# Two transformer blocks on one core: the opening with the first three input-projection units abreast, and another order of its first fetches

## What is computed

```python
# first block
cs = jax.nn.silu(c)
mod = cs @ w_ada[l] + b_ada[l]
shift1, scale1, gate1, shift2, scale2, gate2 = [m[:, None, :] for m in jnp.split(mod, 6, axis=-1)]
h = _rmsnorm(x, norm1_g[l]) * (1.0 + scale1) + shift1
proj = h @ w_in[l]
...
# second block: keys and values of its memory, which depend on nothing in the first block
mem_n = rmsnorm(mem, g_mem)
k_m, v_m = jnp.split(mem_n @ w_mem_kv, 2, axis=-1)
k = rmsnorm(k_m.reshape(bsz, m, MEM_HEADS, MEM_HEAD_DIM), memk_gain)
```

## Time and profile before

| | |
|---|---|
| median of three runs | 814.39 us (814.33 to 815.30) |
| the profiled execution's own time | 814.49 us |
| its span, first to last instruction | 812.7 us |
| TensorE busy | 800.6 us, 99% |
| VectorE busy | 625.6 us, 77% |
| ScalarE busy | 439.7 us, 54% |
| mean granted TensorE clock | 0.998 |

### The profile page before, as it was taken

One profiled execution on the slowest core, in us unless ns is written; L12 is line 12 of the kernel. 1 busy time (PEld: TensorE's weight loads), 2 busy tenths in 40 slices (PEclk: granted clock), 3 DMA queues, 4 the chain that ended last, 5 costly groups with the idle time before them and its releaser, 6 DMA issues.

```text
span 812.7 us, 14321 instructions
## 1 busy us (share of the span) xinstructions
PE 800.6 (99%) x5970; PEld 759.5 (93%) x5970; DVE 625.6 (77%) x913; ACT 439.7 (54%) x603; POOL 33.2 (4%) x32
## 2 busy tenths in 40 slices
PE   7899999999999999999999999999999999999998
PEld 7899789999999999999878999999999999999998
DVE  5998999888888887676977686644787876777765
ACT  7838667637555344444857546654436544545351
POOL 1000000000000000000000000000000121111210
PEclk9999999999999999999999999999999999999999
DMA  9996848964536865555454543444444655455501
GB/s 357 423 417 221 356 161 308 360 260 156 211 140 241 310 251 201 202 187 177 156 192 137 190 163 149 156 152 160 156 155 163 237 203 177 162 206 202 177 31 52
DMA packets 25487, 168.99 MB, mean 208 GB/s; under 512 B 2896, under 2 KB 3408, under 8 KB 5840
## 3 DMA queue, kind: packets, MB, share of 16 engines
q1 hardware_dynamic: 25280, 168.08, 56.1%
q10 hardware_dynamic: 144, 0.01, 0.0%
HBM read 167.03 MB, written 1.05 MB: 207 GB/s over the span
## 4 chain that ended last, share of the span: by engine, by line
PE 84%; DVE 9%; DMA 3%; ACT 2%; issue 1%; SPq 0%; DVEq 0%; ACTq 0%
PE ps L1648 57%; PE ps L1679 13%; PE ps L1682 7%; DVE wlo L1001 3%; PE ps L1712 3%; DMA raw<-in_w_in 2%; ACT whi L473 2%; PE ps L1890 1%; PE ps L1861 1%; PE ps L1862 1%; DMA raw<-in_first_unit 1%; PE ps L1923 1%; DVE raw L976 0%; DVE tmp L1570 0%; DVE x L1506 0%
## 5 line engine op out<-in xcount | busy, mean ns | idle before, releaser
L1001 DVE TENSOR_TENSOR wlo<-raw,whi 128x2048 fp32r<-128x2048 f32 (+1 forms) x130 | 290.4, 2239 | 85.8 <-ACT whi L473 82.4
L473 ACT ACTIVATE whi<-raw 128x2048 fp32r<-128x2048 f32 (+2 forms) x140 | 250.7, 1799 | 100.9 <-PE ps L1682 67.0
L1648 PE MATMUL ps<-h_two,whi 128*128 128x256 f32 x1344 | 247.2, 286 | 2.5 <-DVE wlo L1001 2.1
L1648 PEld LDWEIGHTS ps<-h_two,whi 128*128 128x128 f32 x1344 | 210.7, 193 | 4.9 <-DVE wlo L1001 2.3
L1648 PE MATMUL ps<-h_two,wlo 128*128 128x256 f32 x672 | 190.7, 284 | 0.0
L1648 PEld LDWEIGHTS ps<-h_two,wlo 128*128 128x128 f32 x672 | 129.5, 193 | 0.0
L1648 PE MATMUL ps<-fhi,whi 128*128 128x256 f32 x352 | 99.6, 283 | 0.0
L1648 PE MATMUL ps<-flo,whi 128*128 128x256 f32 x352 | 99.6, 283 | 0.0
L1648 PE MATMUL ps<-fhi,wlo 128*128 128x256 f32 x352 | 99.6, 283 | 0.0
L1648 PEld LDWEIGHTS ps<-fhi,wlo 128*128 128x128 f32 x352 | 67.6, 192 | 0.0
L1648 PEld LDWEIGHTS ps<-fhi,whi 128*128 128x128 f32 x352 | 67.6, 192 | 0.0
(11 more groups left out here) (260 smaller groups left out, 1328.2 us busy)
## 6 DMA issues: line engine op xcount, KB each, us to landing
raw<-in_w_up SPq DMA_DIRECT2D x44, 1024.0 KB, 4.8
raw<-in_w_in SPq DMA_DIRECT2D x43, 1024.0 KB, 4.8
raw<-in_w_down SPq DMA_DIRECT2D x22, 1024.0 KB, 4.8
raw<-in_w_ada SPq DMA_DIRECT2D x14, 1024.0 KB, 5.4
raw<-in_branches SPq DMA_DIRECT2D x10, 1024.0 KB, 5.4
raw<-in_w_out SPq DMA_DIRECT2D x4, 1024.0 KB, 7.3
raw<-in_w_o SPq DMA_DIRECT2D x4, 1024.0 KB, 4.8
raw<-in_w_mem_kv SPq DMA_DIRECT2D x3, 1024.0 KB, 9.0
```

The lines of the kernel that those rows point to most:

```text
L473: return nc.scalar.activation(dst, src, func, **kw)
L1001: V.tensor_tensor(wlo[:, w % SPLIT, c:UNIT], raw[:, slot, c:UNIT], f32(whi[:, w % SPLIT, c:UNIT]), ALU.subtract).then_inc(raw_done, 1)
L1648: ins = mm(out_, l, r, start=start and i == 0, stop=stop and i == 2, **kw)
```

## The change

Four things are edited, all in the opening; the same computation is done, by the same instructions but for one unit's split.

- `START_PLAN`: unit 3 is fetched ahead of piece 1, and unit 5 ahead of piece 3.
- `HALVED` takes in unit 6 (`WIN1 + 2`), so that ScalarE rounds it in two instructions and VectorE subtracts in two.
- `START_STEPS`: units 4, 5 and 6 do their tiles 0 to 2 one unit after the other, then all three do tile 3, then unit 7 does its tiles 0 to 3. Before, only units 4 and 5 did so, and unit 6 did its four tiles after them.
- ScalarE's and VectorE's lists follow suit: unit 3 is rounded ahead of `memory_keys`, unit 5 is subtracted ahead of piece 3, and ScalarE's `first_tile(4)` stands ahead of the rounding of unit 7 and no longer behind it.

```diff
@@ -76,9 +76,9 @@
 
 FIRST = 4
 MEMKV, WIN1, BR1, WO1, FFN1 = 0, 4, 21, 25, 29
-START_PLAN = [("w", 0), ("w", 1), ("w", 2), ("ada", 0), ("ada", 1), ("w", 3), ("ada", 2), ("w", 4), ("ada", 3), ("w", 5),
+START_PLAN = [("w", 0), ("w", 1), ("w", 2), ("ada", 0), ("w", 3), ("ada", 1), ("ada", 2), ("w", 4), ("w", 5), ("ada", 3),
               ("w", 6), ("ada", 4), ("w", 7), ("ada", 5), ("ada", 6), ("ada", 7), ("ada", 8)]
-HALVED = (MEMKV + 1, MEMKV + 2, MEMKV + 3, WIN1 + 3, WIN1 + FIRST, WIN1 + FIRST + 1)
+HALVED = (MEMKV + 1, MEMKV + 2, MEMKV + 3, WIN1 + 2, WIN1 + 3, WIN1 + FIRST, WIN1 + FIRST + 1)
 WIN2, BR2, WO2, FFN2 = 62, 88, 94, 98
 NW = 131
 PLAN, RAW_OF = build_plan()
@@ -118,8 +118,7 @@
 SCORE_BANK, PT_BANKS, PV_BANK = 4, (3, 6), 7
 TURN_BANK = 4
 ROWS_BANK = 4
-START_STEPS = ([(0, kt) for kt in range(3)] + [(1, kt) for kt in range(3)] + [(0, 3), (1, 3)]
-               + [(2, kt) for kt in range(4)] + [(3, kt) for kt in range(4)]
+START_STEPS = ([(w, kt) for w in range(3) for kt in range(3)] + [(w, 3) for w in range(3)] + [(3, kt) for kt in range(4)]
                + [(w, kt) for kt in (4, 5, 6, 7) for w in range(FIRST)])
 
 NORMS = {"mem": (KT, 0, 3, 3), "one": (KT, 0, 6, 6), "two": (KT, 0, 4, 4), "final": (KT, 0, 3, 6), "mix": (KT, 0, 3, 3),
@@ -606,25 +605,25 @@
             act.wait_ge(sem("one_rstd"), 1)
             for tt in range(NT):
                 copy(xn[:, tt, :], xt[:, tt, :], scale=rstd[:, c_one + tt:c_one + tt + 1]).then_inc(sem("xn_ready"), 1)
+            round_unit(MEMKV + 3)
             memory_keys(0)
             memory_keys(1)
-            round_unit(MEMKV + 3)
             act.wait_ge(sem("vec_landed"), 16)
             first_tile(0)
-            first_tile(1)
             act.wait_ge(emptied["act"], EVACUATED[MEMKV + 1][1])
             copy(memk_sq[:, :, :], kmem[:, :, :], ACT.Square).then_inc(sem("memk_sq"), 2)
+            first_tile(1)
+            memory_values(0)
             round_unit(WIN1)
             first_tile(2)
-            memory_values(0)
             round_unit(WIN1 + 1)
             memory_values(1)
-            first_tile(3)
-            round_unit(WIN1 + 2)
             act.wait_ge(sem("memk_mean"), 1)
             copy(memk_saved, ps[:, NORMS["memk"][2], 0:8]).then_inc(sem("memk_saved"), 1)
+            round_unit(WIN1 + 2)
+            first_tile(3)
+            first_tile(4)
             round_unit(WIN1 + 3)
-            first_tile(4)
             act.wait_ge(sem("lam_dots"), 2)
             copy(lam_e, lam_d, ACT.Exp).then_inc(sem("lam_exp"), 1)
             first_tile(5)
@@ -1136,17 +1135,20 @@
             invert("one")
             dve.wait_ge(sem("cs_ready"), 1)
             first_gain(0)
+            split_low(MEMKV + 3, fold=False)
             first_gain(1)
-            split_low(MEMKV + 3, fold=False)
             first_low(0)
+            first_gain(2, 0)
             first_low(1)
-            first_gain(2)
+            first_gain(2, 1)
             split_low(WIN1, fold=False)
             first_low(2)
-            first_gain(3)
             split_low(WIN1 + 1, fold=False)
+            first_gain(3, 0)
+            split_low(WIN1 + 2, fold=False, half=0)
+            first_gain(3, 1)
+            split_low(WIN1 + 2, fold=False, half=1)
             first_low(3)
-            split_low(WIN1 + 2, fold=False)
             first_gain(4)
             split_low(WIN1 + 3, fold=False, half=0)
             first_low(4)
```

## The result

The changed kernel takes 817.85 us (median of five runs, 817.66 to 818.34) against 814.39, a ratio of 1.0047 with a 95% interval of 1.0036 to 1.0057. The profiled execution took 818.34 us, 3.85 more than the one of before (814.49).

The account below looks back on a forecast made before the run. TensorE, busy 99%, bounds the kernel; unit 8's start is the measure. Unit 7 at 49.3, 17 steps to 61.5, slow stretch to 63.3, plus 2.46 gives 65.8, +2.6: 817.0 us, range 814.2 to 818.9.

Parts of the forecast that it names:

- The walk to unit 7: TensorE's opening: waits of 0.7, 0.4 and 0.7 us, then a 3.7 us pause until unit 7 at 49.3.
- low 7: VectorE's low part of tile 7, in its tail: expected at 60.4, which is 57.99 + 2.4.
- the price of the one slow stretch seen before: TensorE behind the pause before unit 7: the clock falls once more, costing 1.76 us as before.
- the stated bounds of 0 and 3.5: Limits on the slow stretch's cost: 0 if the clock stays up, 3.5 us if low twice as long.
- the 65.8 of the sum: Start of unit 8 on TensorE: 63.3 for unit 4's end plus 2.46, against 63.19 before, so +2.6.
- The clock stayed up: Rival, TensorE behind unit 7's pause: no slow stretch, VectorE's 64.4 sets unit 8, +1.2, 815.6 us; chance 0.15.
- The transfers landed in their new order: Rival, opening fetches: transfers don't land in issue order, unit 5 lands at 35.7, +4.4, 818.8 us; chance 0.07.
- The gain case: Rival, opening: unit 7's half ready before about 48.2, pause only 1.3 us, 813.3 us or less; chance 0.11.
- the 62.1: Start of unit 8 in the rival where the opening gains: 57.99 + 2.8 + 1.2, or -1.1.
- taken up later: Rival, chain after 63.19: spare time there absorbs a late unit 8, 814.4 us; chance 0.07.

Follow-up runs that it names:

- the first two experiments: Changed kernel with ScalarE rounding unit 7 ahead of tile 4: 813.89 us, 0.9999 of before; kernel before with tile 4 ahead of that rounding: 817.20 us, 1.0034.
- the first experiment: Changed kernel with one line moved back, so ScalarE rounds unit 7 ahead of tile 4: 813.89 us, 0.9999 of before.

## Why the prediction was right, and where it was off

**The walk to unit 7 held.** The wait before unit 3 went. The next waits came out at 0.35, 0.80 and 0.51 us for 0.7, 0.4 and 0.7, the pause before unit 7 at 3.44 for 3.7, its end at 49.65 for 49.3, VectorE's idle time at 2.03 for 2.2, low 7 at 60.64 for 60.4. That ScalarE's order makes this pause was shown from both sides, by the first two experiments.

**The clock was mis-sized.** I took the price of the one slow stretch seen before, 1.76 us; it cost 14.91 - 12.24 = 2.67 this time, inside the stated bounds of 0 and 3.5. The stretch was 6.8 us long and not 3.4; about 1.3 of it lay in the pause and cost nothing. With 0.35 for the start of unit 7 and 0.91 for the clock, the 65.8 of the sum becomes 67.06; measured 67.03. Where the clock fell is told by a finer stretch:

```profile
48.00:50.00 2.00, 0.35 (x1) 0.35 (x2) 1.63 (x3) 1.98 (x3) 0.00 (x0) 0.58 1.03 430
```

It was at 1.2 GHz for 2 x 0.42 x 2 = 1.7 of these 2 us, so from 48.3, and unit 7 began at 49.65. In time: 817.85 against 817.0, the range (814.2 to 818.9) and the sign held. The median is nearer to the forecast than unit 8 is, because the profiled execution was the slowest of the five, 0.49 above it.

**The base was not one number.** The profiled execution of before belongs to the group with the slow stretch (median 814.70), and I took it for all. So the forecast rested the fall of the clock on one execution in which it fell, where, by their mean clocks, it stayed up in 38 of 72; that it fell in all five of the changed kernel is more than the rows of before could tell. Against the other group (813.48) the changed kernel is 4.4 us slower.

**The rivals.** The clock stayed up in none of the changed kernel's five runs (mean clock 0.998 in two, at 817.66 and 817.85, and 0.996 in three, at 817.81 to 818.34); forced up, it gives 815.91, where this rival stood at 815.6. The transfers landed in their new order: ScalarE rounded unit 3 at 23.10, and its only wait for DMA between units 4 and 7 was the one for unit 6. The gain case needed unit 7's half by 48.2; moved there (TensorE began unit 7 at 47.54 in the first experiment, after the pause of 1.3 us that this rival gave) the kernel ties with before, 0.5 behind the 62.1 and 0.6 behind the 813.3 of the rival. Nothing was taken up later.

**What I had not weighed** is the place of an idle time. The forecast asked whether the clock falls; the run with the old step order shows that where it falls decides whether it costs anything.

## What to carry to other kernels

When a list written out by hand is rearranged for one engine's sake, go through every other engine's list for the instruction that now stands behind a wait it doesn't need: here two instructions moved ahead of a rounding whose data had already landed cost 0.47%. Where TensorE must wait for another engine anyway, let it wait early, ahead of work that has slack, rather than right before the stretch that sets the end. A split or a reorder pays only if it shortens the longest of the ways to the next stage; compare them first, since two of them may be equally long.

## What the runs showed of the hardware

A pause of TensorE of one and the same length lowered its clock in some executions and not in others. The 2.1 us before unit 5 did so in the profiles of the kernel before (2.11) and of the one with piece 8 split (2.10), and did not in that of the kernel before with tile 4 first (2.11). The pause of 2.09 us before unit 7 there was followed by a slow stretch, the one of 2.16 us before tile 5 with pieces 4 and 8 split was not. By the mean clocks the kernel before had a slow stretch in 34 of 72 executions. In the profiles here the clock stayed at 2.4 GHz behind pauses of 0.5 to 1.3 us and fell to 1.2 GHz with those of 3.11 and 3.44 us.

A long pause is not the only way there: with pieces 4 and 8 split the clock fell near 36 us behind sixteen matmuls of 128x1 and an idle time of 0.18 us. These small matmuls stand there in every kernel here, and in the other profiles the clock stayed up behind them. What makes the difference is open.

The clock stayed low for 3.4 us or, in the changed kernel's profile, 6.8. By the mean clocks three of its five executions had more time at 1.2 GHz than the other two (0.996 against 0.998), yet their median is only 0.2 us longer. Why it is not more is not shown, since none of the other two was profiled.

Matmuls without a use kept the clock up where they filled the pause: 16 of them in all 22 executions of two kernels, 28 of them in seven of ten, while the other three had a slow stretch that cost nothing. They took 1.9 us off the changed kernel and brought the kernel before to the times of its better group.
